# Five norms of a hybrid encoder: sums of squares turned in 32x32 blocks by the vector engine

## The reference, cut to what matters

```python
def rmsnorm(x, g):
    return x * lax.rsqrt(jnp.mean(x * x, axis=-1, keepdims=True) + EPS) * g

for i in range(2):
    h = rmsnorm(x, norm1_g[i])
    x = x + (attention(h) if i == 0 else retention(h))
    h = rmsnorm(x, norm2_g[i])
    x = x + conv_ffn(h)          # (gelu(a) * b) @ w_down, a and b after a width-3 convolution
# retention, for each of 4 heads, o: 512 tokens x 512
o = o * lax.rsqrt(jnp.mean(o * o, axis=-1, keepdims=True) + EPS)
out += (silu(g) * o) @ w_o
```

## Time and profile before

| | us |
|---|---|
| median of 3 runs | 1268.42 |
| lowest, highest | 1268.1, 1268.46 |
| profiled execution, its own time | 1268.73 |
| its span, first to last instruction | 1266.5 |
| PE busy | 1259.6 (99%) |
| DVE busy | 713.5 (56%) |
| ACT busy | 465.4 (37%) |
| POOL busy | 141.8 (11%) |
| the 64 recorded matmuls of `columns` (L1310), busy | 7.6 |
| the 64 weight loads for them, busy | 8.4 |
| the 6 transposes of `root_row` (L1317), busy | 1.6 |
| granted TensorE clock, mean | 1.000 |

### The profile page before, as it was taken

The page is one execution under the profiler, slowest core; times in us unless marked ns, Lnnn a source line. Parts: engine busy times, 40 slices in busy tenths (PEclk is TensorE's granted clock), DMA queues, the critical chain, the costliest instruction groups (busy, mean ns, idle before and its releaser), DMA issues.

```text
span 1266.5 us, 15563 instructions
## 1 busy us (share of the span) xinstructions
PE 1259.6 (99%) x5858; PEld 1041.7 (82%) x5858; DVE 713.5 (56%) x906; ACT 465.4 (37%) x655; POOL 141.8 (11%) x138
## 2 busy tenths in 40 slices
PE   9999999999999999999999999999999999999999
PEld 8777888888888888888888888888888888888887
DVE  6776576677664333545535634634676677663221
ACT  5654454444442223233233223223454444442120
POOL 3651300000000001402102201201000000000000
PEclk9999999999999999999999999999999999999999
DMA  6102232222222323312222222221232222222322
GB/s 244 68 34 69 98 108 99 99 98 86 86 80 96 103 91 135 145 68 100 95 79 75 99 99 75 100 69 65 100 108 99 99 92 88 87 80 96 106 91 89
DMA packets 21909, 120.43 MB, mean 95 GB/s; under 512 B 2680, under 2 KB 3728, under 8 KB 11120
## 3 DMA queue, kind: packets, MB, share of 16 engines
q1 hardware_dynamic: 20928, 117.72, 26.5%
q10 hardware_dynamic: 720, 1.85, 0.4%
q0 software_dynamic: 224, 0.35, 0.1%
HBM read 117.81 MB, written 2.11 MB: 95 GB/s over the span
## 4 chain that ended last, share of the span: by engine, by line
PE 99%; DMA 0%; ACT 0%; DVE 0%; ACTq 0%; issue 0%
PE ps L1293 32%; PE ps L1295 32%; PE ps L1294 32%; PE ps L1413 1%; PE ps L1391 1%; PE ps L1400 1%; PE ps L1310 0%; DMA raw<-in_w_kv 0%; PE ps L1374 0%; PE ps L1364 0%; PE ps L1323 0%; ACT va L404 0%; DVE h_lo L662 0%; DVE x L945 0%; PE ps L1317 0%; ACT h_hi L348 0%
## 5 line engine op out<-in xcount | busy, mean ns | idle before, releaser
L1293 PE MATMUL ps<-h_hi,w_hi 128*128 128x512 f32 x960 | 375.3, 391 | 0.0
L1295 PE MATMUL ps<-h_hi,w_lo 128*128 128x512 f32 x960 | 373.6, 389 | 0.0
L1294 PE MATMUL ps<-h_lo,w_hi 128*128 128x512 f32 x960 | 373.5, 389 | 0.0
L657 DVE TENSOR_TENSOR w_lo<-raw,w_hi 128x2048 fp32r<-128x2048 f32 (+1 forms) x115 | 244.3, 2124 | 141.8 <-ACT w_hi L344 141.8
L344 ACT ACTIVATE w_hi<-raw 128x2048 fp32r<-128x2048 f32 (+1 forms) x115 | 202.6, 1762 | 211.9 <-PE ps L1295 211.9
L1293 PEld LDWEIGHTS ps<-h_hi,w_hi 128*128 128x128 f32 x960 | 180.3, 188 | 37.5
L1295 PEld LDWEIGHTS ps<-h_hi,w_lo 128*128 128x128 f32 x960 | 180.2, 188 | 37.6
L1294 PEld LDWEIGHTS ps<-h_lo,w_hi 128*128 128x128 f32 x960 | 180.3, 188 | 36.6
L1295 PE MATMUL ps<-g_hi,w_lo 128*128 128x512 f32 x352 | 136.9, 389 | 0.0
L1293 PE MATMUL ps<-g_hi,w_hi 128*128 128x512 f32 x352 | 136.9, 389 | 0.0
L1294 PE MATMUL ps<-g_lo,w_hi 128*128 128x512 f32 x352 | 136.9, 389 | 0.0
(11 more groups left out here) (161 smaller groups left out, 1431.7 us busy)
## 6 DMA issues: line engine op xcount, KB each, us to landing
raw<-in_w_up SPq DMA_DIRECT2D x44, 1024.0 KB, 4.8
raw<-in_w_ret SPq DMA_DIRECT2D x32, 1024.0 KB, 4.8
raw<-in_w_dn SPq DMA_DIRECT2D x32, 704.0 KB, 4.0
raw<-in_w_ao SPq DMA_DIRECT2D x4, 1024.0 KB, 4.6
raw<-in_w_q SPq DMA_DIRECT2D x3, 1024.0 KB, 5.3
x<-in_xT SPq DMA_DIRECT2D x8, 256.0 KB, 5.1
out<-x SPq DMA_DIRECT2D x8, 256.0 KB, 5.0
rbc<-root_mem SPq DMA_DIRECT2D x6, 256.0 KB, 3.1
```

What stands on the lines that cost most here:

```text
L657: nc.vector.tensor_tensor(w_lo[:, s, 0:cols], raw[:, s, 0:cols], w_hi[:, s, 0:cols].bitcast(F32), ALU.subtract).then_inc(w_lo_ok, 1)
L1293: nc.tensor.matmul(dst, st[0], mv[0], start=start, stop=False)
L1294: nc.tensor.matmul(dst, st[0], mv[1], start=False, stop=False)
L1295: return nc.tensor.matmul(dst, st[1], mv[0], start=False, stop=stop)
```

## The change

For five of the eight norms (both feed-forward norms and the first three heads) the sum over partitions is made otherwise:

- `cross_sums`: DVE turns `ssum` in blocks of 32x32 (one STREAM_TRANSPOSE, 128x512), so that a partition holds tokens and the free axis holds 32 features of a block. A reduction then adds each 32, into `part`, 128x16. DVE does this where `variance` stood, behind the same split of a weight unit.
- `cross_columns`: PE adds the four groups of 32 partitions with one float32 product, stationary `sel` (128x32, made once at the start from the identity), moving `part` (128x16). The result is 32x16: token 32c+j stands in row j, column c.
- `cross_variance` on DVE and `cross_root` on POOL work on 32x16 values.
- `cross_row`: PE turns 32x16 into 16x32 with one float32 product against the identity, and ACT and SP carry `root` as 16 rows of 32 values.

The new PE steps stand later. In a feed-forward layer the row is turned at `k == 6`. In a head the gate tile 2 is made in one piece, PE waits for `part` before tile 3, and the row is turned after seven steps of tile 3.

```diff
-            def spread(row, which):
+            def spread(row, which, crossed=True):

                 sp.wait_ge(row_ok, row + 1)
-                sp.dma_start(root_mem, root[:, :]).then_inc(row_out, 16)
+                if crossed:
+                    sp.dma_start(root_mem.rearrange("t (c j) -> (t c) j", j=XT), root[:, 0:XT]).then_inc(row_out, 16)
+                else:
+                    sp.dma_start(root_mem, root[0:PT, :]).then_inc(row_out, 16)
...
+            def cross_sums(n, squares):
+                dve.wait_ge(ssum_ok, squares)
+                nc.vector.transpose(sq[:, 0, :], ssum[:, :]).then_inc(turn_ok, 1)
+                dve.wait_ge(turn_ok, n + 1)
+                nc.vector.tensor_reduce(part[:, 0, :], sq[:, 0, :].rearrange("p (c i) -> p c i", i=XT), AX.X,
+                                        ALU.add).then_inc(part_ok, 1)
+
+            def cross_variance(n, width, bank=6):
+                dve.wait_ge(col_done, n + 1)
+                nc.vector.tensor_scalar(part[0:XT, 1, :], ps[0:XT, bank, 0:XB], 1.0 / width, EPS, ALU.mult,
                                         ALU.add).then_inc(var_ok, 1)
...
+                nc.vector.tensor_reduce(sel[:, :], ident[:, :].rearrange("p (b j) -> p j b", j=XT), AX.X,
+                                        ALU.add).then_inc(sel_ok, 1)
...
                     if first and s == 0:
-                        variance(ST_F1 if layer else ST_F0, 0, D)
+                        cross_sums(CROSS_F1 if layer else CROSS_F0, SQ_BASE[NORM_F1 if layer else NORM_F0] + KT)
+                        cross_variance(ST_F1 if layer else ST_F0, D)
                         split(up + j + 1, s, cols)
...
+            def cross_root(n):
+                pool.wait_ge(var_ok, n + 1)
+                nc.gpsimd.tensor_tensor(part[0:XT, 2, :], part[0:XT, 1, :], mhalf[0:XT, 0:XB], ALU.pow).then_inc(r_ok, 1)
...
+            def cross_columns(bank=6):
+                nc.tensor.matmul(ps[0:XT, bank, 0:XB], sel[:, :], part[:, 0, :], start=True,
+                                 stop=True).then_inc(col_done, 1)
+
+            def cross_row(bank=7):
+                nc.tensor.matmul(ps[0:XB, bank, 0:XT], part[0:XT, 2, :], ident[0:XT, 0:XT], start=True,
+                                 stop=True).then_inc(row_done, 1)
...
-                            if first and s == 1 and ab == 0 and k == 2:
-
-                                root_row(ST_F1 if layer else ST_F0, 0)
+                            if first and s == 1 and ab == 0 and k == 6:
+
+                                pe.wait_ge(r_ok, (ST_F1 if layer else ST_F0) + 1)
+                                cross_row()
...
                         if first and s == 0 and ab == 1:
-                            columns(ST_F1 if layer else ST_F0, SQ_BASE[norm] + KT)
+                            pe.wait_ge(part_ok, (CROSS_F1 if layer else CROSS_F0) + 1)
+                            cross_columns()
...
-                gate_part(2, 0, 6)
-                pe.wait_ge(gx_ok, 4 * h + 2)
-                columns(ST_HEAD + h, SQ_HEAD + 4 * (h + 1), bank=4)
-                gate_part(2, 6, KT).then_inc(g_done, 1)
-                gate_part(3, 0, 1)
...
                 else:
-                    root_row(ST_HEAD + h, 1, bank=5)
-                gate_part(3, 1, KT).then_inc(w_used, 1)
+                    gate_part(2, 0, KT).then_inc(g_done, 1)
+                    pe.wait_ge(gx_ok, 4 * h + 2)
+                    pe.wait_ge(part_ok, CROSS_HEAD + h + 1)
+                    gate_part(3, 0, 1)
+                    cross_columns(bank=4)
+                    gate_part(3, 1, 6)
+                    pe.wait_ge(r_ok, ST_HEAD + h + 1)
+                    gate_part(3, 6, 7)
+                    cross_row(bank=5)
+                    gate_part(3, 7, KT).then_inc(w_used, 1)
```

More of the change, by code:

```diff
@@ L79 @@
 ST_A, ST_F0, ST_R, ST_HEAD, ST_F1 = 0, 1, 2, 3, 3 + R_HEADS
+XT = 32
+XB = S // XT
+CROSS_F0, CROSS_HEAD, CROSS_F1 = 0, 1, R_HEADS
 ROW_F0, ROW_R, ROW_HEAD, ROW_F1 = 0, 1, 2, 1 + R_HEADS
@@ L110, in trunk @@
         rbc = sb("rbc", [P, 2, S])
-        root = sb("root", [PT, P])
+        root = sb("root", [XB, P])
+        sel = sb("sel", [P, XT])
+        part = sb("part", [P, 4, XB])
         ps = ctx.enter_context(nc.psum_tensor("ps", [P, 8, S], F32))
@@ L199, in trunk @@
         col_done, var_ok, r_ok, bc_done, bc_ok = (sem(n) for n in ("col_done", "var_ok", "r_ok", "bc_done", "bc_ok"))
+        sel_ok, turn_ok, part_ok = (sem(n) for n in ("sel_ok", "turn_ok", "part_ok"))
         row_done, row_ok, row_out, row_in = (sem(n) for n in ("row_done", "row_ok", "row_out", "row_in"))
@@ L317, in _ @@
                     load(w_ret[2 * j + s], PAIR_RET + j, s, UW)
-            spread(ROW_R, 0)
+            spread(ROW_R, 0, crossed=False)
             for j in range(2, 4):
@@ L363, in broadcast_out, with root_out @@
                 nc.scalar.activation(rbc[:, which, :], ps[:, bank, :], ACT.Copy).then_inc(bc_ok, 1)
-            def root_out(row, bank=7):
+            def root_out(row, bank=7, crossed=True):
                 act.wait_ge(row_done, row + 1)
-                nc.scalar.activation(root[:, :], ps[0:PT, bank, 0:P], ACT.Copy).then_inc(row_ok, 1)
+                if crossed:
+                    nc.scalar.activation(root[:, 0:XT], ps[0:XB, bank, 0:XT], ACT.Copy).then_inc(row_ok, 1)
+                else:
+                    nc.scalar.activation(root[0:PT, :], ps[0:PT, bank, 0:P], ACT.Copy).then_inc(row_ok, 1)
             act.wait_ge(warm_ok, 1)
@@ L635, in _ @@
             act.dma_start(dec[:, :, :], decay).then_inc(r_in, 16)
-            root_out(ROW_R)
+            root_out(ROW_R, crossed=False)
             qkvg(0, True)
@@ L670, in variance @@
                 nc.vector.tensor_scalar(var[:, which, :], ps[:, bank, 0:PT], 1.0 / width, EPS, ALU.mult,
+                                        ALU.add).then_inc(var_ok, 1)
+            def cross_sums(n, squares):
[7 more added lines that the diff above has]
+                nc.vector.tensor_scalar(part[0:XT, 1, :], ps[0:XT, bank, 0:XB], 1.0 / width, EPS, ALU.mult,
                                         ALU.add).then_inc(var_ok, 1)
@@ L1038, in qkvg @@
                 split(pv + 2, 0, UW)
-                variance(ST_HEAD + h, 1, R_V, bank=4)
+                if final:
+                    variance(ST_HEAD + h, 1, R_V, bank=4)
+                else:
+                    cross_sums(CROSS_HEAD + h, SQ_HEAD + 4 * h + 4)
+                    cross_variance(ST_HEAD + h, R_V, bank=4)
                 dve.wait_ge(g_done, h + 1)
@@ L1262, in _ @@
             nc.gpsimd.memset(u[:, :, 0:2], 0.0).then_inc(cst, 1)
-            inv_root(ST_F0, 0)
+            cross_root(ST_F0)
             add_squares(SQ_BASE[NORM_R], KT)
@@ L1270, in _, with qkvg @@
                 nc.gpsimd.tensor_tensor(csr[:, i, :], tab[:, i, :], rbc[:, 0, :], ALU.mult).then_inc(csr_ok, 1)
-            def qkvg(h, first):
+            def qkvg(h, final=False):
                 for s in range(2):
@@ L1278, in qkvg @@
                 add_squares(SQ_HEAD + 4 * h, RV_T)
[L1279 to L1283, removed]
+                if final:
+                    inv_root(ST_HEAD + h, 1)
+                else:
+                    cross_root(ST_HEAD + h)
+            with pool.Fori(0, R_HEADS - 1) as h:
+                qkvg(h)
+            qkvg(R_HEADS - 1, True)
             pool.wait_ge(w_used, 2 * PAIR_UP[1])
             nc.gpsimd.memset(u[:, :, 0:2], 0.0).then_inc(cst, 1)
-            inv_root(ST_F1, 0)
+            cross_root(ST_F1)
         @block.tensor
@@ L1679, in qkvg @@
                 pe.wait_ge(vlo_ok, 4 * h + 4)
-                gate_part(2, 0, 6)
-                pe.wait_ge(gx_ok, 4 * h + 2)
-                columns(ST_HEAD + h, SQ_HEAD + 4 * (h + 1), bank=4)
-                gate_part(2, 6, KT).then_inc(g_done, 1)
-                gate_part(3, 0, 1)
-                if final:
+                if final:
+                    gate_part(2, 0, 6)
+                    pe.wait_ge(gx_ok, 4 * h + 2)
+                    columns(ST_HEAD + h, SQ_HEAD + 4 * (h + 1), bank=4)
+                    gate_part(2, 6, KT).then_inc(g_done, 1)
+                    gate_part(3, 0, 1)
                     broadcast(ST_HEAD + h, 1, bank=5)
+                    gate_part(3, 1, KT).then_inc(w_used, 1)
                 else:
-                    root_row(ST_HEAD + h, 1, bank=5)
-                gate_part(3, 1, KT).then_inc(w_used, 1)
+                    gate_part(2, 0, KT).then_inc(g_done, 1)
+                    pe.wait_ge(gx_ok, 4 * h + 2)
+                    pe.wait_ge(part_ok, CROSS_HEAD + h + 1)
+                    gate_part(3, 0, 1)
+                    cross_columns(bank=4)
[4 more added lines that the diff above has]
+                    gate_part(3, 7, KT).then_inc(w_used, 1)
             def project(h, p):
```

## The result

The changed kernel took 1279.97 us (median of 5 runs, 1279.54 to 1280.0) where the kernel before took 1268.42 us (5 runs): ratio 1.0089, 95% interval 1.0078 to 1.01. It is **11.5 us slower**. The forecast was 1267.7 us in a range of 1265.5 to 1270.3: off by 12 us and outside the range, with no rival that comes near. In the profiled executions (1268.73 and 1279.54 us by their own times) the span went from 1266.5 to 1277.3 us. The granted clock of TensorE is 1.0 in both, its upper level (2.4 GHz), so no clock explains it.

The account below looks back on a forecast made before the run. The prediction took PE, with 99% of the chain, as the bound. Heads -1.5 us and feed-forward norms +0.8 gave -0.7, from 1268.73 to 1268.0 profiled, 1267.7 us as the runs' median; range 1265.5 to 1270.3.

## What to carry to other kernels

When a change adds or resizes any buffer, work out what it does to the distance between the moving and the stationary operand of the large matmuls, and pad it to a multiple of 256 bytes if it moves; an unused tensor of the same size in the old kernel tells in one run whether placement is the cause. A step that is moved to hide a wait must be followed to its users on the other engines, and their reserve read from the rows: here 12 matmuls of moving cost more than the new steps saved. A small product's price is read from a row with the same number of weight columns and the same type, and where there is none, the upper bound has to leave room for an idle time ahead of its load (0.35 us here).

## What the runs showed of the hardware that was not expected

- A 128x512 matmul in a dense stream starts 0.2267 us after the one before if the distance between its operands is the kernel before's or 256, 512 or 1024 bytes more, and 0.2333 us after it for shifts of 32, 96, 128, 192, 224 and 384; at 64 it is 0.229. Over this kernel that is up to 18.6 us (1287.69 against 1269.11). The distance from `w_hi` to `g_hi` in the kernel before is itself a multiple of 256. The cause in the chip stays open.
- A float32 product of 16 or 32 weight columns has an idle time of 0.35 us ahead of its load and costs 0.37 us; one of 128 columns costs 0.25, and a transpose with 16 columns about 0.1. The reason is open.
- A power on POOL takes 2.90 us for 16 columns on 32 partitions and 2.907 on 128.
